# The first feed-forward product of a two-block model: half-block products for 13 of 16 pairs of hidden tiles, mixed with the second product

## The reference, cut to what matters

```python
h = rmsnorm(x, norm_mlp_w[l]) * (1.0 + sc2) + sh2
ff = jnp.square(jax.nn.relu(h @ mlp_w1[l])) @ mlp_w2[l]     # 1024 -> 4096 -> 1024
x = x + g2 * ff                                             # g2: a part of silu(c) @ ada_w + ada_b
return rmsnorm(x, final_norm_w)                             # then the second block
```

## Time and profile before

| | |
|---|---|
| time, median of 3 runs | 1275.32 us (1275.16 to 1275.36) |
| profiled execution, first to last instruction | 1272.2 us; the runs' time holds some 3 us around it |
| TensorE busy | 1239.2 us, 97% |
| VectorE busy | 837.0 us, 66% |
| ScalarE busy | 580.9 us, 46% |
| GpSimd busy | 93.5 us, 7% |
| feed-forward stage | about 324 to 674 us |

### The profile page before, as it was taken

The page is one execution under the profiler, slowest core; times in us unless marked ns, Lnnn a source line. Parts: engine busy times, 40 slices in busy tenths (PEclk is TensorE's granted clock), DMA queues, the critical chain, the costliest instruction groups (busy, mean ns, idle before and its releaser), DMA issues.

```text
span 1272.2 us, 18645 instructions
## 1 busy us (share of the span) xinstructions
PE 1239.2 (97%) x6580; PEld 1014.3 (80%) x6580; DVE 837.0 (66%) x1270; ACT 580.9 (46%) x841; POOL 93.5 (7%) x144
## 2 busy tenths in 40 slices
PE   4999999999999999999999999999999999999998
PEld 3777778788888888888888888888888887777786
DVE  6889997857765333444444887665466668987822
ACT  3675445534444122433332655333233346978723
POOL 7022210000000000000000000110010000100000
PEclk9999999999999999999999999999999999999999
DMA  9688853426465333332333232334232232333321
GB/s 367 189 198 170 180 109 98 131 63 189 133 181 148 91 93 98 100 98 84 99 99 86 80 91 85 89 99 116 83 98 83 83 113 69 105 102 91 100 66 67
DMA packets 197981, 147.17 MB, mean 116 GB/s; under 512 B 6490, under 2 KB 178705, under 8 KB 197920
## 3 DMA queue, kind: packets, MB, share of 16 engines
q1 hardware_dynamic: 190448, 134.40, 35.4%
q0 software_dynamic: 6272, 10.91, 4.6%
q10 hardware_dynamic: 1200, 1.05, 0.3%
HBM read 135.59 MB, written 2.10 MB: 108 GB/s over the span
## 4 chain that ended last, share of the span: by engine, by line
PE 72%; DVE 16%; ACT 6%; issue 4%; DMA 1%; POOL 1%; DVEq 0%; ACTq 0%; SPq 0%; POOLq 0%
PE banks L421 22%; PE banks L423 22%; PE banks L422 22%; DVE w_lo L405 2%; ACT w_hi L393 2%; DVE score L1979 1%; DVE m L1976 1%; DVE xc L2513 1%; POOL e L2718 1%; DMA x_tok<-in_x 1%; DVE vh L2413 1%; DVE score L1962 1%; DMA hq<-in_ada_w 1%; PE banks L1119 1%; DVE sqb L1911 1%
## 5 line engine op out<-in xcount | busy, mean ns | idle before, releaser
L405 DVE TENSOR_TENSOR w_lo<-raw,w_hi 128x1024 fp32r<-128x1024 f32 x200 | 243.8, 1223 | 142.8 <-ACT w_hi L393 137.8
L421 PE MATMUL banks<-h_hi,w_hi 128*128 128x512 f32 x792 | 318.1, 402 | 2.3 <-DVE w_lo L405 0.8
L423 PE MATMUL banks<-h_hi,w_lo 128*128 128x512 f32 x792 | 309.0, 390 | 0.0
L422 PE MATMUL banks<-h_lo,w_hi 128*128 128x512 f32 x792 | 308.8, 390 | 0.0
L393 ACT ACTIVATE w_hi<-raw 128x1024 fp32r<-128x1024 f32 x200 | 209.6, 1052 | 195.4 <-PE banks L423 162.0
L421 PEld LDWEIGHTS banks<-h_hi,w_hi 128*128 128x128 f32 x792 | 148.8, 188 | 42.3 <-issue 8.3
L422 PEld LDWEIGHTS banks<-h_lo,w_hi 128*128 128x128 f32 x792 | 148.9, 188 | 33.4 <-issue 3.8
L423 PEld LDWEIGHTS banks<-h_hi,w_lo 128*128 128x128 f32 x792 | 148.8, 188 | 31.2
L421 PE MATMUL banks<-n_hi,w_hi 128*128 128x512 f32 x288 | 113.6, 395 | 0.9 <-DVE e L2475 0.9
L422 PE MATMUL banks<-n_lo,w_hi 128*128 128x512 f32 x288 | 112.3, 390 | 0.0
L423 PE MATMUL banks<-n_hi,w_lo 128*128 128x512 f32 x288 | 112.3, 390 | 0.0
(11 more groups left out here) (415 smaller groups left out, 1817.8 us busy)
## 6 DMA issues: line engine op xcount, KB each, us to landing
raw<-in_mlp_w SPq DMA_DIRECT2D x64, 512.0 KB, 3.9
raw<-in_a_w_in SPq DMA_DIRECT2D x48, 512.0 KB, 3.8
raw<-in_w_in SPq DMA_DIRECT2D x28, 512.0 KB, 4.4
raw<-in_ada_w SPq DMA_DIRECT2D x26, 512.0 KB, 4.6
raw<-in_b_w_in SPq DMA_DIRECT2D x24, 512.0 KB, 3.7
raw<-in_a_w_out SPq DMA_DIRECT2D x16, 512.0 KB, 3.7
raw<-in_b_w_out SPq DMA_DIRECT2D x12, 512.0 KB, 3.6
raw<-in_w_out SPq DMA_DIRECT2D x8, 512.0 KB, 4.3
```

The costliest lines, as they stand in the source:

```text
L405: dve.tensor_tensor(dst, src, hi, ALU.subtract).then_inc(split_lo, 1)
L421: pe.matmul(dst, l_hi, r_hi, start=first, stop=False, skip_group_check=onto)
L422: pe.matmul(dst, l_hi, r_lo, start=False, stop=False, skip_group_check=onto)
L423: return pe.matmul(dst, l_lo, r_hi, start=False, stop=last, skip_group_check=onto)
```

## The change

The hidden tiles are made in another way and in another order, written out item by item (`ITEMS`) instead of in loops.

The first six tiles stay whole: 24 products of 512 columns each. The other 26 are made in 13 pairs. A pair is a 2 x 2 block product: weights A11 to A22 (two tiles by two halves of the 1024 input channels), values B11 to B22 (two halves of the channels by two halves of the tokens). Seven products of half blocks replace eight, each of 4 x 3 matmuls of 256 columns. They need four sums of weight blocks for each pair (S1 to S4, on GpSimd) and four of value blocks once (T1 to T4, on GpSimd; ScalarE and VectorE make their high and low parts). The outputs share products: ScalarE copies three of a pair's partial results out of PSUM (`snap`) while TensorE goes on adding to the bank, and VectorE adds these copies to other banks (`block`).

Between the parts of a pair stand four items of the second product (`down`): a group of four hidden tiles by one channel row, 12 products of 512 columns, added onto x at once. The rings hold eight half units instead of four units; the hidden tiles are kept for two groups of four.

```diff
+HIDDEN, GROUP, WHOLE = D_FF // P, 4, 6
+FORM = {1: "A11", 2: "A12", 3: "S4", 4: "A22", 5: "S1", 6: "S2", 7: "S3"}
+for _p in range(FIRST_PAIR, PAIR_END):
+    ITEMS += [("part", _p, 1), ("part", _p, 2), _down[0], ("part", _p, 5), _down[1], ("part", _p, 6), _down[2],
+              ("part", _p, 7), _down[3], ("part", _p, 3), ("part", _p, 4)]
+    RAWS += [("w1", 2 * _p), ("w1", 2 * _p + 1)] + [("w2", _down[_n][1], _down[_n][2] // 2) for _n in (0, 2)]
...
# SyncE: one list of loads, the gate's tiles in between
+            for m, what in enumerate(RAWS):
+                if m < RING:
+                    sp.wait_ge(split_lo, U_FF - RING + m + 1)
+                else:
+                    raw_free(m - RING)
...
+                sp.dma_start(raw[:, r, :].rearrange("p (k n) -> p k n", n=src.shape[2]), src).then_inc(raw_in[r], 16)
+                for t in {3: (0, 1), 4: (2,), 5: (3,), 6: (4,), 7: (5,), 8: (6,), 9: (7,)}.get(m, ()):
+                    sp.wait_ge(g2_used, t + 1)
+                    sp.dma_start((ada_a, ada_b)[t % 2][:, :], a["ada_w"][0, t * P:(t + 1) * P, 5 * D:6 * D]).then_inc(side_in[t % 2], 16)
+            def raw_free(m):
...
+                if kind == "w2":
+                    sp.wait_ge(f_lo, max(SLOT["down", g, 2 * RAWS[m][2] + n] + size_of(("down", g, 2 * RAWS[m][2] + n)) for n in range(2)))
+                elif g < WHOLE:
+                    sp.wait_ge(f_lo, SLOT["whole", g] + 2)
+                else:
+                    sp.wait_ge(f_lo, SLOT["part", g // 2, 4 if g % 2 else 2] + 1)
+                    sp.wait_ge(ff_summed, sum_count(g // 2, "S4"))
...
# TensorE
+            def part(p, i):
+                pe.wait_ge(f_lo, SLOT[item] + 1)
+                if i == 1 and p < FIRST_PAIR + 2:
+                    pe.wait_ge(evac, E_FF + 3 * (p % 2) + 3)
...
+                if i == 6:
+                    pe.wait_ge(ff_added, added(p, 1))
+                if i == 4:
+                    pe.wait_ge(ff_added, added(p, 2))
+                for k in range(4):
+                    m_hi, m_lo = value(i, k)
+                    last = three(pe, part_bank(p, i), hi[:, k * P:(k + 1) * P], lo[:, k * P:(k + 1) * P], m_hi, m_lo,
+                                 i in (1, 2, 5) and k == 0, k == 3, True)
...
+                if item == ("down", 0, 0):
+                    second_gate_columns()          # waits for all eight gate tiles
...
# ScalarE, item by item; `now` are the half units whose ring slots the item frees
+            for item, now in made_at():
+                for what in now:
+                    slot_hi(act, what)
+                if kind == "whole":
+                    used(act, item)
+                    act.activation(zt[:, g % 4, :], banks[:, g, :], ACT.Relu).then_inc(evac, 1)
+                    squared(g)
...
# VectorE
+            for item, now in made_at():
+                for what in now:
+                    slot_lo(dve, what)
+                if kind == "whole":
+                    if g:
+                        hidden_low(g - 1)
+                    gate_tile(g)
+                elif kind == "part":
+                    if i == 1:
+                        if g == FIRST_PAIR:
+                            hidden_low(WHOLE - 1)
+                            gate_tile(6)
+                            gate_tile(7)
+                            form_lows((0, 1))
...
+                    if i == 7:
+                        block(g, 7, zt[:, 2 * g % 4 + 1, HALF:], 1, 2)
...
# GpSimd: six operations for each of four channel tiles, then four sums for each pair
+            for p in range(FIRST_PAIR, PAIR_END):
+                raw_wait(pool, ff_raw(RAWS.index(("w1", 2 * p))))
+                raw_wait(pool, ff_raw(RAWS.index(("w1", 2 * p + 1))))
+                for name, left, right, op in (("S1", a21, a22, ALU.add), ("S2", sum_at("S1"), a11, ALU.subtract),
+                                              ("S3", a11, a21, ALU.subtract), ("S4", a12, sum_at("S2"), ALU.subtract)):
+                    pool.tensor_tensor(sum_at(name), left, right, op).then_inc(ff_summed, 1)
```

More of the change, by code:

```diff
@@ new lines, in is_sum, with sum_at, sum_count, size_of @@
+        def is_sum(item):
+            return item[0] == "part" and FORM[item[2]][0] == "S"
+        def sum_at(name):
+            return wsums[:, S_ORDER.index(name), :]
+        def sum_count(p, name):
+            return N_TSUM + 4 * (p - FIRST_PAIR) + S_ORDER.index(name) + 1
+        def size_of(item):
+            return 2 if item[0] == "whole" or item == LAST_ITEM else 1
+        def in_slot(ring, item):
+            t = slot(ring, SLOT[item], 2 if item[0] == "whole" else 1)
+            return t.rearrange("p (k n) -> p k n", n=P) if item[0] == "down" else t
@@ new lines, in made_at @@
+        def made_at():
+            made, at = 2 * LEAD, 0
+            coming = [item for item in ITEMS if SLOT[item] >= made]
+            left = [(SLOT[item] + (2 if item[0] == "whole" else 1), item) for item in coming]
+            left += [(SLOTS_END + 2 * j + 2, ("value", j)) for j in range(LEAD)]
+            for item in ITEMS:
+                free = SLOT[item] + SLOTS
+                now = [what for end, what in left if made < end <= free]
+                made = max(made, free)
+                yield item, now
@@ new lines, in _ @@
+            wa = a["a_w_in_2"][0]
+            for j in range(RING):
+                raw_free(len(RAWS) - RING + j)
+                r = raw_index(U_V + j) % RING
+                sp.dma_start(raw[:, r, :].rearrange("p (k n) -> p k n", n=512),
+                             rows(wa, 2 * P * j, 2 * P * (j + 1))[:, :, A_WIDTH:A_WIDTH + 512]).then_inc(raw_in[r], 16)
+            stream(U_V + RING, 12, lambda i, j: (rows(wa, 2 * P * j, 2 * P * (j + 1))[:, :, bass.ds(i * 512 + A_WIDTH + 512, 512)], 512))
@@ L1026, in _ @@
             last.then_inc(ws_summed, 1)
-            def ff_unit(half, j, i=0):
-                u = U_FF + 32 * half + j
-                pe.wait_ge(split_lo, u + 1 + RING * i)
-                pe.wait_ge(evac, E_FF + 16 * half + j - 3 + RING * i)
-                for k in range(KT):
-                    last = three(pe, banks[:, j, :], unit(w_hi, u, P)[:, k, :], unit(w_lo, u, P)[:, k, :],
-                                 h_hi[:, k, :], h_lo[:, k, :], k == 0, k == KT - 1)
-                last.then_inc(w_used, 1)
@@ new lines, in _ @@
+            pe.wait_ge(x_new, X_FF)
+            for k in range(KT):
+                pe.wait_ge(h_ready, H_FF + k + 1)
+                for t in range(3):
+                    if k == 0:
+                        pe.wait_ge(f_lo, SLOT["whole", t] + 2)
+                    last = whole(t, k)
+                    if k == KT - 1:
+                        last.then_inc(f_used, 2)
+            for item in ITEMS[3:]:
+                if item[0] == "whole":
+                    t = item[1]
+                    pe.wait_ge(f_lo, SLOT[item] + 2)
+                    if t >= 4:
+                        pe.wait_ge(wsum_made, t - 3)
+                    for k in range(KT):
+                        last = whole(t, k)
+                    last.then_inc(f_used, 2)
+                elif item[0] == "part":
+                    part(item[1], item[2])
+                else:
+                    down(item[1], item[2])
+                if item == ("down", 0, 0):
+                    second_gate_columns()
```

477 lines of the change are left out of this document (358 added, 119 removed).

## The result

The changed kernel takes **1302.68 us** (median of 4 runs, 1301.63 to 1308.72) beside 1275.34 us for the kernel before on the same chip: ratio 1.0222, 95% interval 1.0199 to 1.0245. It is 27.3 us slower; the forecast was 1295, the range 1275 to 1315, the forecast's own band 1288 to 1303.

A forecast was written before the change was run, and what follows sets the result against it. TensorE was taken to bound the feed-forward stage, busy for all 350.2 us. Saving and waits sum to +7.6 us, GpSimd beside VectorE adds 4.8 at the start and 7.6 in pairs: 1275.3 becomes 1295 us, range 1275 to 1315.

The forecast's parts named there:

- rival (b): Pairs and start: both GpSimd sums fall on the round at up to 1.29 us, start loses 6 to 7; 1313 us, chance 0.20.
- 13 pairs on TensorE: Hidden tiles: 84 products of 256 columns at 119.8 ns replace 48 of 512, 0.82 us less a pair, saving 10.6 us.
- first wait: TensorE before the first 256-column part: waits 8.2 us for the sixth tile's relu; GpSimd beside VectorE adds 4.8.
- second wait, less what the slow parts ahead of it hide: TensorE before the gate's columns: waits 6.3 us more, until the last gate tiles are done at 377.
- part 4 of the first pair: First pair: part 4 waits about 0.5 us for VectorE's block sum behind the late second-layer low.
- half clock behind the second wait: Gate's sixteen column products run slow after idling: 1.7 us added once, bounds 0 and 3.4.
- pairs: Other pairs: a 20.75 us round plus 0.83 for GpSimd is 0.6 over TensorE's 20.95, x 12 = 7.6 us.
- tail: Last group: its first product waits 1.5 us for the low of tile 31; later rows cost 0, at most 2.
- The chain at the start: Start: loads stand behind gate tiles in SyncE's list; without GpSimd gate(3) ends 355.5, sixth relu 365.1, TensorE waits 8.2 us.
- Rival (c): Start: gate tiles don't hold the loads, load 8 issued before 346 us, both long waits vanish; 1267 us, chance 0.10.
- of the other two [sums] I let one fall on the round: Pairs: of four GpSimd weight sums two run while VectorE waits; one of the others lengthens the round by 0.83 us.
- (a): Rival: GpSimd costs nothing, the chain at the start alone decides, pairs 20.95 us apart; 1283 us, chance 0.22.

The follow-up runs named there:

- e4: Changed kernel with GpSimd's 24 value-sum operations cut to 8 columns each, so GpSimd is idle beside VectorE at the start; 1298.04 us, ratio 1.0179.
- e1: Changed kernel with four gate buffers and the gate's tiles moved behind other loads, whole computation kept; 1300.58 us, ratio 1.0197.
- e6: e2 plus unread products on TensorE, 40 ahead of the first pair's wait and 17 ahead of the gate's columns; 1288.81 us, ratio 1.0099.
- e2: Changed kernel with each pair's two second-layer loads ahead of its second first-layer tile, from the second pair on; 1290.03 us, ratio 1.0117.
- e12: e10 with VectorE's block sum and rows ahead of next-pair lows, gate's columns later, two banks exchanged; 1275.69 us, ratio 1.0002.
- e5: Changed kernel with e1's four gate buffers and e4's short value sums together; 1293.20 us, ratio 1.0130.
- e10: Kernel with e2's load order and a reordered start (five gate buffers, later gate), now using that load order in the first pair too; 1276.99 us, ratio 1.0008.

## Why the prediction was right, and where its sizes were off

The direction and the places were right, and the time is in the range. That it also lies in the forecast's own band is luck: it is 0.3 us inside the end of it, rival (b) begins there, and the terms were off by more than that in both directions. The places are two waits at the start, ended by ScalarE's relu and by VectorE's multiply-add, half clock behind them, pairs held by the block sum that part 4 awaits. The sum of the profiled execution, term by term:

| term | predicted | measured |
|---|---|---|
| 13 pairs on TensorE | -10.6 | -10.6 at 119.8 ns, and +1.3 (a 512-column item between parts takes 2.75, not 2.72) |
| first wait | 8.2, and 4.8 for GpSimd | 369.24 - 357.93 - 0.23 = 11.1 |
| second wait, less what the slow parts ahead of it hide | 6.3 | 4.7 + 1.5 = 6.2 |
| part 4 of the first pair | 0.5 | none |
| half clock behind the second wait | 1.7 (0 to 3.4) | 1.6 + 1.3 + 1.1 = 4.0 |
| pairs | 7.6 | 14.5 (13.4 at part 4 of ten pairs, 1.1 at the item of 651.15 for a late low) |
| tail | 1.5 | 1.3 |
| start of the stage | 0 | 1.2 |
| all | 20.0 | 29.0 of the 29.2 us |

In the third line, 4.7 is 381.10 - 376.15 - 0.23, and 1.5 is what the first two parts took beyond full speed (4.4 us from 369.24 on, against 2.9).

**The chain at the start** came as worked out: gate(1) 345.6 forecast and 347.8 measured, load 6 346.1 and 348.2, gate(3) 355.5 and 359.9, the sixth relu 365.1 and 369.1. The drift of 4.4 us at gate(3) is less than the 4.8 that the prediction put down to GpSimd, and not all of it is GpSimd's: from the start of the stage gate(3) ends after 34.5 us here and after 31.4 in e4, without GpSimd's work. So GpSimd cost this chain some 3.1 us, and the first wait 2.9 (10.9 against 8.0); the 8.2 worked out without it is what e4 shows. What the prediction did not see is that GpSimd's own lateness is a second chain of nearly the same length: it changes nothing in the sum, and everything for a mending (e1). Rival (c) fell: load 8 went out at 360.3, not before 346.

**The half clock** was under-sized: it was taken from one row of sixteen columns and put at 1.7 once, bounds 0 to 3.4. It also took the part and the item behind the columns, 2.4 us more, outside the bounds. That the slow parts behind the first wait cost nothing of their own is borne out by e6.

**The round** was the term most off: 22.44 us a pair, not 21.6, beside a TensorE that itself needs 21.08 and not 20.95 (7 x 1.44 + 4 x 2.75). The prediction's pieces against the round shown above: load to copy 5.5 and 5.5; copy 0.65 and 0.66; from the first low to the second block sum's end 4.5 + 0.83 and 580.78 - 574.50 = 6.3; the two stretches of ScalarE and VectorE behind it 3.8 + 6.3 and 3.6 + 6.1. So the step that failed in size is "of the other two [sums] I let one fall on the round": three lows met three sums, 1.8 us instead of 0.83. It is paid in ten pairs, the third to the twelfth; the first two, behind the late start, lose nothing. This puts the pairs between the forecast and rival (b), whose 24 it did not reach; (a) is ruled out by the pair time. The prediction saw that behind the tile's load in SyncE's list stands the second-layer load, and took it as given; e2 shows that this piece of order alone is worth the whole term.

**The tail** and the step of 120 ns held. The start of the stage is 1.2 us later (325.40 against 324.23). In the profiled executions of e1 to e12, with the same instructions ahead of it, it lies between 324.08 and 327.07, so executions alone differ by more than this term; of the kernel before there is one trace, and whether the change has a part in it stays open.

What stays open: whether the 7.6 us of waits left in e12 are VectorE's sum of work or again its order. From 324 to 382 us, where 2.2 us of them lie, VectorE is busy for 56.39 of 58.00 us; taking work off it there (the gate's eight multiply-adds, some 10 us) was not tried. The longest wait, 2.4 us ahead of the second pair's S2 part, looks like order: from 389.6 to 393.3 VectorE idles for 3.0 us for ScalarE's copies, and these stand behind a relu for which ScalarE waited 3.75 us on VectorE's block sum of 389.21. No run tests that.

## What to carry to other kernels

A saving on the busiest engine is worth what the others can follow: here 0.82 us a pair came with a round of four engines that had 0.2 us to spare, and every piece of that round then counted in full. When a stall has one cause on the critical chain, look for the second chain just behind it before mending: e1 took the first chain away and gained 2.1 us by the medians, within noise; e5 took both and gained 9.5. In a list of loads that wait for their slots, put each load where its slot comes free, not where its data belongs: here that was worth 12.7 us (e2).

## What the runs showed of the hardware

A VectorE step with two operands in SBUF and a GpSimd sum on SBUF excluded each other to the end of the instruction: in the changed kernel each stretched low ended 0.54 to 0.56 us behind the GpSimd sum that it had met, in all ten rounds from 440 to 647 us, while the 45 rows onto x, with one operand in PSUM, kept 0.74 to 0.75 us. This had been an estimate from two rows.

In these traces the clock fell around the gate's sixteen products of one column where TensorE had idled just ahead of them. With 1.8 us of idling (e6) they took 3.47 us, and the clock was 0.57 over the 8 us from 382 on, though 17 full products stood ahead of the idling. With 0.56 us (e10) they took 1.95, and the clock was 0.50 from 383 to 395. With none they took 1.84, and the clock stayed at 1.00: in the kernel before, and in e12, where several waits of 0.7 to 2.4 us stand apart from them. Which share of it is the idling's and which the columns', no run separates.
